# A hybrid encoder trunk on one core: weight halves of the expert loop split by one instruction on each of two engines

## What is computed

```python
def swiglu(h, w_in, w_out):
    a, b = jnp.split(h @ w_in, 2, axis=-1)
    return (jax.nn.silu(a) * b) @ w_out
...
    for e in range(N_EXPERTS):
        y = y + gates[:, e:e + 1].astype(hf.dtype) * swiglu(hf, w_in[e], w_out[e])
```

## Time and profile before

| | |
|---|---|
| median of three runs | 1656.91 us |
| the profiled execution | 1656.74 us, of which the span of its instructions is 1655.0 us |
| TensorE matmul busy | 94% of the span |
| VectorE busy | 85%, 1537 instructions |
| ScalarE busy | 65%, 1164 instructions |
| read from memory | 499.28 MB, 302 GB/s over the span |
| the expert loop at full rate | 659 to 1626 us |

### The profile page before, as it was taken

The page is one execution under the profiler, slowest core; times in us unless marked ns, Lnnn a source line. Parts: engine busy times, 40 slices in busy tenths (PEclk is TensorE's granted clock), DMA queues, the critical chain, the costliest instruction groups (busy, mean ns, idle before and its releaser), DMA issues.

```text
span 1655.0 us, 22753 instructions
## 1 busy us (share of the span) xinstructions
PE 1562.3 (94%) x7324; PEld 1296.9 (78%) x7324; DVE 1407.4 (85%) x1537; ACT 1074.0 (65%) x1164; POOL 59.6 (4%) x47
## 2 busy tenths in 40 slices
PE   5999997999979896999999999999999999999996
PEld 4788775888869665888888888888888888888884
DVE  6988987788887745898998998998998998999994
ACT  3454433444355535787787787787887877878783
POOL 0212200000000110000000000000000000000000
PEclk9999998999989996999999999999999999999998
DMA  9977776788847321899999999999999999999991
GB/s 333 348 249 263 253 272 219 254 309 297 317 164 268 102 77 51 325 388 347 358 376 345 359 368 355 358 372 356 349 376 348 358 379 343 362 373 338 366 380 53
DMA packets 235114, 500.91 MB, mean 303 GB/s; under 512 B 9744, under 2 KB 40640, under 8 KB 235072
## 3 DMA queue, kind: packets, MB, share of 16 engines
q1 hardware_dynamic: 233904, 500.29, 83.9%
q10 hardware_dynamic: 1168, 0.07, 0.0%
HBM read 499.28 MB, written 1.05 MB: 302 GB/s over the span
## 4 chain that ended last, share of the span: by engine, by line
PE 83%; DVE 8%; issue 3%; DMA 2%; ACT 2%; POOL 1%; DVEq 0%; SPq 0%; ACTq 0%; POOLq 0%
PE ps L492 24%; PE ps L494 24%; PE ps L493 24%; DVE w_lo L1358 2%; DVE acc L1377 2%; DMA ada<-in_ada_w 2%; PE ps L908 1%; PE ps L726 1%; PE ps L730 1%; PE ps L728 1%; DMA raw<-in_ret_w_in 1%; PE ps L525 1%; PE ps L917 1%; PE ps L941 0%; PE ps L918 0%
## 5 line engine op out<-in xcount | busy, mean ns | idle before, releaser
L1358 DVE TENSOR_TENSOR w_lo<-raw,w_hi 128x1024 fp32r<-128x1024 f32 x834 | 994.2, 1230 | 83.5 <-ACT w_hi L1006 69.4
L1006 ACT ACTIVATE w_hi<-raw 128x1024 fp32r<-128x1024 f32 x834 | 865.6, 1060 | 254.7 <-PE ps L494 216.8
L492 PE MATMUL ps<-w_hi,RA 128*128 128x512 f32 x1528 | 607.2, 397 | 12.0 <-DVE w_lo L1358 2.9
L494 PE MATMUL ps<-w_hi,RA 128*128 128x512 f32 x1528 | 598.5, 392 | 0.0
L493 PE MATMUL ps<-w_lo,RA 128*128 128x512 f32 x1528 | 597.9, 391 | 0.0
L492 PEld LDWEIGHTS ps<-w_hi,RA 128*128 128x128 f32 x1528 | 288.7, 189 | 71.5 <-issue 3.2
L494 PEld LDWEIGHTS ps<-w_hi,RA 128*128 128x128 f32 x1528 | 288.5, 189 | 61.6
L493 PEld LDWEIGHTS ps<-w_lo,RA 128*128 128x128 f32 x1528 | 288.9, 189 | 58.4 <-issue 0.5
L492 PE MATMUL ps<-w_hi,hT_hi 128*128 128x512 f32 x400 | 160.6, 401 | 7.7 <-DVE hT_lo L1428 6.9
L494 PE MATMUL ps<-w_hi,hT_lo 128*128 128x512 f32 x400 | 157.4, 393 | 0.0
L493 PE MATMUL ps<-w_lo,hT_hi 128*128 128x512 f32 x400 | 157.3, 393 | 0.0
(11 more groups left out here) (232 smaller groups left out, 1021.7 us busy)
## 6 DMA issues: line engine op xcount, KB each, us to landing
raw<-in_moe_w_in SPq DMA_DIRECT2D x224, 1024.0 KB
raw<-in_moe_w_out SPq DMA_DIRECT2D x112, 1024.0 KB
ada<-in_ada_w SPq DMA_DIRECT2D x46, 1024.0 KB, 7.3
raw<-in_ff_w_in SPq DMA_DIRECT2D x44, 512.0 KB
raw<-in_ret_w_in SPq DMA_DIRECT2D x16, 1024.0 KB
raw<-in_ff_w_out SPq DMA_DIRECT2D x11, 1024.0 KB
raw<-in_ret_w_in SPq DMA_DIRECT2D x16, 512.0 KB
raw<-in_ret_w_out SPq DMA_DIRECT2D x8, 1024.0 KB
```

The source lines that it names most:

```text
L492: pe.matmul(out, a_hi, b_hi, start=first, stop=False)
L494: return pe.matmul(out, a_lo, b_hi, start=False, stop=last)
L1006: act.activation(w_hi[:, cn % RING, cols], raw[:, cn % RAW, cols], ACT.Copy).then_inc(hi_done, 1)
L1358: v.tensor_tensor(w_lo[:, cn % RING, cols], raw[:, cn % RAW, cols], w_hi[:, cn % RING, cols].bitcast(f32), ALU.subtract).then_inc(lo_done, 1)
```

## The change

In the expert loop a half is split by one instruction of 2048 columns on each of the two engines (`split_half`), where there were two of 1024. On ScalarE it waits until TensorE has used both quarters of the slot; on VectorE until ScalarE's whole half is done; the semaphores are raised by 2 at its end. The first four halves of the loop and the last two keep the quarters, as do all other stages. Since a half is now indivisible, the order changes where a half was cut by other work: all of c+8 now stands behind `tile_high` on ScalarE and behind `tile_low` on VectorE, and ahead of `y_high` and `y_low`; the last quarter of c+2 at the start of a step is gone, since c+2 was completed in the step before.

```diff
--- before.py
+++ after.py
@@ -1008,6 +1008,12 @@
             def split(c, m=0):
                 split_quarters(c, m, 0, 2)
 
+            def split_half(c, m):
+
+                act.wait_ge(w_in[c % RAW], 32 * (c // RAW + 1) + 32 * m)
+                act.wait_ge(w_used, before_half(c - RING + 1, m))
+                act.activation(w_hi[:, c % RING, :], raw[:, c % RAW, :], ACT.Copy).then_inc(hi_done, 2)
+
             def root_mean_square(n):
 
                 act.activation(stat[:, 18:19], eps[:, :], ACT.Sqrt)
@@ -1297,16 +1303,19 @@
             def step(j, me, ne, more=True):
 
                 c, n = U_MOE + 4 + RAW * (j - 1), me + j
-                split_quarters(c, me, 5, 9)
+                split_half(c + 3, me)
                 act.wait_ge(eg_ok, n)
+                split_half(c + 4, me)
                 tile_silu(n, c + 2, me)
-                split_quarters(c, me, 9, 12)
+                split_half(c + 5, me)
                 if j < ET - 1 or more:
-                    split_quarters(c, me, 12, 14)
+                    split_half(c + 6, me)
                     if j == ET - 1:
                         gathered_high(ne + 1)
-                    split_quarters(c, me, 14, 17)
+                    split_half(c + 7, me)
                 tile_high(n)
+                if j < ET - 1 or more:
+                    split_half(c + 8, me)
                 if j == ET:
                     y_high(ne)
                 if j == 2:
@@ -1326,8 +1335,10 @@
                 gathered_high(NE * p)
                 split(U_MOE + 3, m0)
                 tile_silu(m0, U_MOE + 2, m0)
-                split_quarters(U_MOE + 4, m0, 0, 5)
+                split_half(U_MOE + 4, m0)
+                split_half(U_MOE + 5, m0)
                 tile_high(m0)
+                split_half(U_MOE + 6, m0)
                 step(1, m0, NE * p)
                 with act.Fori(0, NE - 1) as e:
                     ne = NE * p + e
@@ -1360,6 +1371,12 @@
 
             def split(c, m=0):
                 split_quarters(c, m, 0, 2)
+
+            def split_half(c, m):
+
+                dve.wait_ge(hi_done, before_half(c + 1, m))
+                v.tensor_tensor(w_lo[:, c % RING, :], raw[:, c % RAW, :], w_hi[:, c % RING, :].bitcast(f32),
+                                ALU.subtract).then_inc(lo_done, 2)
 
             def ada_steps(u, first, end, k=0):
 
@@ -1801,22 +1818,23 @@
             def step(j, me, ne, e, more=True):
 
                 c, n = U_MOE + 4 + RAW * (j - 1), me + j
-                split_quarters(c, me, 5, 9)
+                split_half(c + 3, me)
                 if j == ET + 1:
                     accumulate(ne, e)
-                split_quarters(c, me, 9, 12)
-                if j < ET - 1 or more:
-                    split_quarters(c, me, 12, 13)
+                split_half(c + 4, me)
+                split_half(c + 5, me)
                 dve.wait_ge(eT_done, n)
                 tile_product(n, c + 4, me)
                 if j < ET - 1 or more:
-                    split_quarters(c, me, 13, 14)
+                    split_half(c + 6, me)
                     if j == ET - 1:
                         gathered_low(ne + 1)
-                    split_quarters(c, me, 14, 17)
+                    split_half(c + 7, me)
                 if j == ET:
                     y_gated(ne, c + 6, me)
                 tile_low(n)
+                if j < ET - 1 or more:
+                    split_half(c + 8, me)
                 if j == ET:
                     y_low(ne)
                 if j == ET - 3 and more:
@@ -1835,10 +1853,11 @@
                     one_hot(NE * p, 0)
                 gathered_low(NE * p)
                 split(U_MOE + 3, m0)
-                split_quarters(U_MOE + 4, m0, 0, 1)
+                split_half(U_MOE + 4, m0)
                 tile_product(m0, U_MOE + 4, m0)
-                split_quarters(U_MOE + 4, m0, 1, 5)
+                split_half(U_MOE + 5, m0)
                 tile_low(m0)
+                split_half(U_MOE + 6, m0)
                 step(1, m0, NE * p, 0)
                 with dve.Fori(0, NE - 1) as e:
                     ne = NE * p + e
```

## The result

| | before | changed |
|---|---|---|
| median of 5 runs, us | 1655.64 (1653.4 to 1657.97) | 1663.0 (1661.39 to 1664.13) |
| profiled execution, us | 1656.74 | 1662.66 |
| its span, us | 1655.0 | 1661.0 |
| one expert, scatter to scatter, us | 122.39 | 123.57 |

The ratio is 1.0043, 95% interval 1.0029 to 1.0058: slower by 7.4 us. That is the forecast's direction, and its 1664.2 us is 1.2 us too high.

What follows compares the result with a forecast made beforehand. TensorE was taken to set the pace of the expert loop, with the splits' savings worth nothing. Seven scatter delays of 1.07 us add 7.5 us to 1656.74, giving 1664.2 us; the range was 1656 to 1672.

Steps and rivals of the forecast that it cites:

- TensorE paces, and what is saved elsewhere is worth nothing: Expert loop: TensorE sets the pace, so 20 us saved on VectorE and 25 on ScalarE count as nothing.
- The instruction times: Loop splits: 2048 columns take 2.29 us on VectorE and 1.93 on ScalarE; instruction counts fall to 1207 and 834.
- The chain in step 7: From ScalarE's c+7 through two VectorE splits to `y_low`: the scatter waits 0.96 us plus 0.11 restart, for seven experts.
- 7 waits of about 0.96: Sign expected in the profile after: the scatter (L941) waits seven times for `y_low` (L1808), about 0.96 us each.
- Behind the wait nothing else becomes late: After the scatter's wait: VectorE's next split and two accumulates have 1.8 us more, and SyncE's transfers don't move.
- The margin of the ordinary step: Split of c+8 in ordinary steps: ready 0.26 us before TensorE needs its weights, so no wait and cost 0.
- The rival built on 0.26: 47 steps with c+8 and no `y_low` behind it: the margin isn't there, total 1669 to 1678 us; chance 0.12.
- Absorbed: Rival at the scatter: the late `y_low` is absorbed, about 1656.7 us, no change; chance 0.17.
- Clock: Rival on TensorE: the granted clock falls at each wait, 1.7 us an expert more, 1676 us; chance 0.03.
- Faster: Rival in the loop: VectorE sets the pace after all and its 20 us are gained, 1637 us; chance 0.04.
- the rule weighed: Skill's advice that grouping operations can improve throughput on a saturated engine: alone it would give 1637 us for VectorE's loop.
- The bounds 1662.3 and 1665.8: Limits of the forecast total in us, from a scatter wait between 0.8 and 1.3 us an expert.

Runs made afterwards that it cites:

- mixed kernel: Changed kernel with whole halves only in steps 2 to 6 of each expert, quarters in the old order in steps 1, 7 and 8: 1654.66 us, ratio 1.0004.
- the 512 columns: Changed kernel with an extra, unread ScalarE copy of 512 columns in each step, ahead of the split of c+8: 1675.42 us, ratio 1.012.

## Why the prediction was right

- **TensorE paces, and what is saved elsewhere is worth nothing.** Right. The mixed kernel saves VectorE 237 x 0.06 us and comes out at 1.0004.
- **The instruction times.** 2.29 and 1.93 were taken, 2.290 and 1.918 measured; the counts are 1207 and 834.
- **The chain in step 7.** Right in place, number and form: seven waits of L941 for L1808. Its size was 0.96 + 0.11 an expert, and 1.04 + 0.11 was measured (1.17 with what the other matmuls add). The 0.08 that it lacked are two hand-overs. ScalarE's c+7 ends at 1032.36 + 1.92 = 1034.28 and VectorE starts at 1034.38, 0.10 later, where I had 0.05. And ScalarE itself starts 0.10 after the matmul that frees the slot (1031.88 + 0.39 to 1032.36), where my 1031.28 was the start of a quarter, 0.04 after it (1030.85 + 0.39). That is 0.11 together; the durations, each within 0.02 of its term, give 0.03 of it back. On VectorE 1036.59, 1037.72, 1038.32 and 1040.52 are 2.21, 1.13, 0.60 and 2.20 apart. The two matmuls, changed and before:

```profile
1031.88 0.39 PE L494 MATMUL ps<-w_hi,RA 128*128 128x512 f32 x1
```

```profile
1030.85 0.39 PE L494 MATMUL ps<-w_hi,RA 128*128 128x512 f32 x1
```

- **The sign that I named, "7 waits of about 0.96".** The view has 0.88. I had worked out a delay between starts, and the view counts idle time between a record's end and a start. The two differ by 0.16, and the second understates.
- **"Behind the wait nothing else becomes late".** True of the changed kernel, since the wait gives VectorE time. That this wait also protected step 8 is what the runs with `y_low` first and without the wait show; I hadn't seen that the two are one shortage.
- **The margin of the ordinary step.** Right in sign: no step is late. Its size was given as 0.26 because the weight load was taken to need the half one matmul earlier. The changed kernel's rows show 0.48 before the matmul's start, and the 512 columns show that all of it but a hand-over can be used: with 0.52 more the matmul started 0.09 late. The rival built on 0.26 was thus weaker than its 0.12. It was no idle worry though: one more microsecond a step on ScalarE adds 37 us here.
- **The other rivals.** *Absorbed*: no; the chain would have had to be 0.96 us shorter, and it was 0.08 longer. *Clock*: 1.00 between 659 and 1632. *Faster*: a TensorE that is 99% busy in the loop took nothing from 24 us less work on VectorE. That is also the rule weighed: grouping gained nothing where VectorE, though 92% busy, ended in time; the trace is on the side of the Trainium skill's second sentence (Perfetto Trace Analysis, Optimizing Scalar/DVE Operations), by which work in pieces can be done sooner.
- **The sum.** 1664.2 against 1663.0. The loop costs 8.2 instead of 7.5, and the two ends of the profiled span took 2.2 back, which no step of the prediction had. So the total is closer than the steps deserve, and that is luck. The bounds 1662.3 and 1665.8 are 7 x 0.8 and 7 x 1.3 alone: I had left the 0.11 of restart out of them, and with it they are 1663.1 and 1666.6.

## What to carry to other kernels

Where one engine paces the loop, as here, ask of a merged instruction on another engine what it does to the latest thing that the pacing engine waits for. It can't start before the last of its inputs and releases nothing before its end, and the microseconds that it saves were worth nothing here. Look for the place with the least reserve, where extra work stands in the queue, here `y_gated`, `y_low` and the accumulates; merge elsewhere if at all, and expect no time for it. And read lateness of TensorE from the starts of its matmuls: the column of waits loses the first 0.16 us of each (matmuls of 512 columns at full clock).

## What the runs showed of the hardware that I had not expected

- A hand-over has several sizes, and they go with how the waiting instruction's wait stands in the program. From ScalarE's split to VectorE's it is 0.03 us with quarters on VectorE, in the kernel before as behind ScalarE's whole halves (1034.27 to 1034.30 above), and 0.10 with whole halves on VectorE (1034.28 to 1034.38). From TensorE's last matmul on a slot to ScalarE's split it is mostly 0.04 with quarters and 0.10 with whole halves. From VectorE to the matmul that waited it is 0.05. The traces have a difference that goes with it: ahead of each large split stands an instruction that does nothing but wait, 330 of them on each engine, and VectorE has none ahead of its quarters. The 30 quarters on ScalarE in the kernel before that do follow such an instruction have 0.10 too. The first row is VectorE's in the changed kernel, the second its quarters' in the kernel before:

```profile
L1377 DVEq EVENT_SEMAPHORE  x330: 21/21/21, 663.2 to 1627.2; - x165
```

```profile
L1357 DVEq ALU_OP  x745: 40/40/52, 86.2 to 1630.4; - x187
```

- 47 late starts of 0.09 us each, with 0.11 of restart behind each, leave no row in the view of waits.
- After the same wait of 2.89 us near the end, TensorE ran at 1.2 GHz for 6.8 us in one kernel's execution and 3.4 in the other's. The last expert is 1.0 us shorter in the second. Why the two differ, and whether the change has a part in it, stays open.
